# The last key search of a sparse attention cut into 18 pieces between its softmaxes, gate tiles moved into its rounds, scores issued in pairs

## What is computed

```python
h = rms_norm(x, g_mix[l]) * (1.0 + sc_m) + sh_m
qa, ka, va, qi, ki, wi, qb, kb, vb, ga, gb = split_cols(h @ w_in[l] + b_in[l])
# sparse attention: the 128 best keys of each query, by an index score, are kept
score = einsum('bqh,bqhs->bqs', wi, relu(qi . ki)) * INDEX_SCALE   # over 8 index heads
sel = top_k(where(admissible, score, -inf), 128)
y_a = softmax(qa . ka over sel) . va  @ w_oa[l]                    # 8 heads, one key/value head
# dense attention with a position bias, 8 heads of their own
y_b = softmax(qb . kb + bias) . vb  @ w_ob[l]
merged = sigmoid(ga) * y_a + sigmoid(gb) * y_b
x = x + gt_m * (merged @ w_out[l])
x = x + gt_f * ((silu(gate) * up) @ w_down[l])                     # gate, up = h2 @ w_gu[l]
```

## Time and profile before

| | us |
|---|---|
| median of 3 runs | 4437.27 (4436.09 to 4440.68) |
| the profiled execution, its own time | 4436.38 |
| its span, first to last instruction | 4434.6 |
| TensorE busy | 4012.5 (90%) |
| DVE / ACT / POOL busy | 1686.6 / 1419.9 / 1400.6 |
| first attention of the second block, layer 0 | 2718.4 to 2852.4 |
| second attention, layer 0 | 2852.4 to 2935.0 |
| first attention, layer 1 | 3667.4 to 3801.3 |

### The profile page before, as it was taken

One profiled execution on the slowest core, in us unless ns is written; L12 is line 12 of the kernel. 1 busy time (PEld: TensorE's weight loads), 2 busy tenths in 40 slices (PEclk: granted clock), 3 DMA queues, 4 the chain that ended last, 5 costly groups with the idle time before them and its releaser, 6 DMA issues.

```text
span 4434.6 us, 66065 instructions
## 1 busy us (share of the span) xinstructions
PE 4012.5 (90%) x28400; PEld 3192.3 (72%) x28400; DVE 1686.6 (38%) x2894; ACT 1419.9 (32%) x2412; POOL 1400.6 (32%) x583
## 2 busy tenths in 40 slices
PE   7798889989988987999899887999999887998999
PEld 5687568877866884678787675677787665787887
DVE  5443341466144444313562357223111475223112
ACT  3344152222223442433222233333222233433222
POOL 4000314344432002234344443023444432043443
PEclk9899899999988997999999997699999995899999
DMA  3001112256220001122363210112222220022222
GB/s 128 2 3 41 55 50 95 93 207 217 95 76 20 3 3 55 58 89 95 148 253 118 95 70 25 38 58 76 109 95 95 76 76 10 29 95 76 95 95 95
DMA packets 37147, 356.72 MB, mean 80 GB/s; under 512 B 4224, under 2 KB 4352, under 8 KB 17920
## 3 DMA queue, kind: packets, MB, share of 16 engines
q1 hardware_dynamic: 19584, 278.93, 16.9%
q10 hardware_dynamic: 17280, 73.60, 4.7%
HBM read 350.42 MB, written 2.10 MB: 79 GB/s over the span
## 4 chain that ended last, share of the span: by engine, by line
PE 80%; DVE 12%; ACT 3%; issue 2%; POOL 2%; DMA 1%; POOLq 0%; DVEq 0%; SPq 0%; PEldq 0%; ACTq 0%; PEld 0%
PE bank L658 20%; PE bank L659 20%; PE bank L660 20%; PE bank L987 11%; PE bank L1962 5%; PE bank L2049 1%; DVE arena L2400 1%; DVE arena L2399 1%; ACT arena L1317 1%; DMA ring<-stream 1%; DVE arena L1762 1%; DVE arena L1665 1%; ACT arena L2104 1%; POOL ring_r L746 1%; ACT hi_ring L737 1%
## 5 line engine op out<-in xcount | busy, mean ns | idle before, releaser
L746 POOL TENSOR_TENSOR ring_r<-ring,hi_ring 128x1024 fp32r<-128x1024 f32 (+1 forms) x522 | 1287.0, 2470 | 2579.5 <-ACT hi_ring L737 2579.4
L658 PE MATMUL bank<-xT_r,ring_r 128*128 128x512 f32 x2288 | 915.3, 400 | 22.9 <-DVE x_lo_r L2469 16.8
L659 PE MATMUL bank<-x_lo_r,hi_ring 128*128 128x512 f32 x2288 | 907.1, 396 | 0.0
L660 PE MATMUL bank<-xT_r,hi_ring 128*128 128x512 f32 x2288 | 903.6, 395 | 0.0
L737 ACT ACTIVATE hi_ring<-ring 128x1024 fp32r<-128x1024 f32 (+1 forms) x522 | 543.4, 1046 | 818.9 <-PE bank L660 392.5
L658 PEld LDWEIGHTS bank<-xT_r,ring_r 128*128 128x128 f32 x2288 | 436.7, 191 | 130.8 <-issue 30.6
L660 PEld LDWEIGHTS bank<-xT_r,hi_ring 128*128 128x128 f32 x2288 | 434.5, 190 | 101.8
L659 PEld LDWEIGHTS bank<-x_lo_r,hi_ring 128*128 128x128 f32 x2288 | 436.7, 191 | 96.6 <-issue 1.8
L987 PE MATMUL bank<-arena 64*64 64x64 f32 (+4 forms) x7456 | 394.6, 250 | 77.6 <-DVE arena L1665 29.6
L1317 ACT ACTIVATE arena<-bank 128x512 f32<-128x512 f32 (+1 forms) x422 | 230.4, 547 | 566.8 <-PE bank L660 359.8
L987 PEld LDWEIGHTS bank<-arena 64*64 64x64 f32 (+2 forms) x7456 | 306.0, 140 | 133.5 <-issue 90.7
(11 more groups left out here) (247 smaller groups left out, 5070.5 us busy)
## 6 DMA issues: line engine op xcount, KB each, us to landing
ring<-stream SPq DMA_DIRECT2D x132, 2048.0 KB, 7.8
arena<-ada ACTq DMA_DIRECT2D x96, 512.0 KB, 4.3
arena<-ln_rows ACTq DMA_DIRECT2D x5, 1024.0 KB, 7.6
arena<-edge ACTq DMA_DIRECT2D x4, 1024.0 KB, 5.0
arena<-edge ACTq DMA_DIRECT2D x2, 1792.0 KB, 7.4
arena<-pack ACTq DMA_DIRECT2D x2, 1548.0 KB, 6.5
arena<-pack ACTq DMA_DIRECT2D x2, 1200.5 KB, 12.7
x<-x_in SPq DMA_DIRECT2D x4, 512.0 KB, 7.3
```

The lines of the kernel that those rows point to most:

```text
L658: first = nc.tensor.matmul(out_, left[1], right[0], start=start, stop=False)
L659: low = nc.tensor.matmul(out_, left[0], right[1], start=False, stop=False)
L660: return first, low, nc.tensor.matmul(out_, left[0], right[0], start=False, stop=stop)
L746: nc.gpsimd.tensor_tensor(feed.raw(n, ring_r), feed.raw(n), feed.hi(n).bitcast(F32), ALU.subtract).then_inc(split_lo, 1)
```

## The change

- The search of the last query tile is cut into 18 pieces (`TOP_STEPS`: scaling, 16 pairs of MAX8 and replacement, mask). They are issued behind the softmaxes of turns 0 to 14 of the first attention, one or two to a turn. Tiles 1 and 2 are searched at one go as before, and the row steps behind them are 10 and 18 instead of 8 and 13, which leaves 8 instead of 15 behind the index scores of tile 3.
- A query tile's first softmax waits for the mask of its own tile instead of all four. ACT's squares of qb and kb wait for the last mask, since they overwrite the scores.
- The norm of qb moves to turns 17 and 18, that of kb to 25 and 27, the transposes of qb to 20, 21, 22 and 24, the load of the first half of the biases (`rel_half`) to turn 30.
- Six gate tiles are early: four in turns 2, 6, 10 and 14 of the first attention, two in turns 2 and 10 of the second. The `gt` steps go from the first attention behind gate tiles 4 to 7 of k = 1. The four `y2_split` steps go behind gate tiles 6 and 7 of k = 0, two each (they stood behind tiles 2 to 5, two of them thus ahead of tile 4).
- In both attentions score products come in pairs: rounds 0 and 1 at the start, then rounds n + 1 and n + 2 at the end of each odd turn n.
- Three regions of memory move with this, and the floor of the first gate piece's split is `idx(3, 0)` instead of `gt(0)`.

```diff
-EARLY_GATES = 4
+EARLY_GATES = 6
+TOP_STEPS = TOPK // 8 + 2
...
-        add("top", qt)
-        more((8, 13, len(rest))[qt - 1])
+        for i in range(TOP_STEPS if qt < TT - 1 else 0):
+            add("top", qt, i)
+        more((10, 18, len(rest))[qt - 1])
...
-        add("s_qk", a, 0, banks=(2,))
+        for n in range(2):
+            add("s_qk", a, n, banks=(2 + n,))
+        top = 0
         for n in range(TT * HQ + 3):
-            if n + 1 < TT * HQ:
-                add("s_qk", a, n + 1, banks=(2 + (n + 1) % 2,))
             if n < TT * HQ:
                 add("s_soft", a, n)
-            if a == 0 and n in (2, 12):
-                add("head_norm", ("qb", "kb")[n // 10], banks=("power",))
-            if a == 0 and n in (5, 15):
-                add("head_scale", ("qb", "kb")[n // 10])
+            while a == 0 and top < min(TOP_STEPS, TOP_STEPS * (n + 1) // (2 * HQ - 1)):
+                add("top", TT - 1, top)
+                top += 1
+            if a == 0 and n in (17, 25):
+                add("head_norm", ("qb", "kb")[n // 25], banks=("power",))
+            if a == 0 and n in (18, 27):
+                add("head_scale", ("qb", "kb")[n // 27])
...
-            if a == 1 and n in (1, 9, 17, 25):
-                add("gate", 0, n // 8, banks=(1,))
-            if a == 0 and n in (3, 5, 7, 14):
-                add("gt", (3, 5, 7, 14).index(n), banks=(1,))
-            if a == 0 and n in (8, 9, 10, 12):
-                add("rows_T", "qb", (8, 9, 10, 12).index(n), banks=(1,))
-            if a == 0 and n == 20:
+            if n in ((2, 6, 10, 14) if a == 0 else (2, 10)):
+                add("gate", 0, n // 4 + 4 * a - a * (n // 10), banks=(1,))
+            if a == 0 and n in (20, 21, 22, 24):
+                add("rows_T", "qb", (20, 21, 22, 24).index(n), banks=(1,))
+            if a == 0 and n == 30:
                 add("rel_half")
             if n >= 3:
                 add("s_pv", a, n - 3)
+            if n % 2 and n + 1 < TT * HQ:
+                for m in (n + 1, n + 2):
+                    add("s_qk", a, m, banks=(2 + m % 2,))
...
-            if n == 0 and dt in (2, 3, 4, 5):
-                add("y2_split", dt - 2)
+            if n == 0 and dt >= EARLY_GATES:
+                for c in range(2):
+                    add("y2_split", 2 * (dt - EARLY_GATES) + c)
+            if n == 1 and dt >= 4:
+                add("gt", dt - 4, banks=(1,))
...
-    return number(with_splits(out, second_pieces(), {24: ("gt", 0), GU_PIECE: ("turn2", 1, 2)}))
+    return number(with_splits(out, second_pieces(), {24: ("idx", 3, 0), GU_PIECE: ("turn2", 1, 2)}))
...
+                    act.wait_ge(mask_ready, TT)
...
-                    dve.wait_ge(mask_ready, TT)
                     drained(dve, uses, "rows_T", "misc", 1)
+                if h == 0 and a == 0:
+                    dve.wait_ge(mask_ready, qt + 1)
```

More of the change, by code:

```diff
@@ L1870, in build @@
     branch2_tmp = region(17200, 2)
-    gates2_early = [arena[:, a_:a_ + S] for a_ in (9232, 9744, W_HI + 4096, 12304)]
+    gates2_early = [arena[:, a_:a_ + S] for a_ in (3088, 3600, 4112, 4624, 12304, 9232)]
     def gate2_at(k, dt):
@@ L1888, in build @@
     mod_slot = [arena[:, 22888 + D * n:22888 + D * n + D] for n in range(MOD_SLOTS)]
-    gt_wide = arena[:, 12560:13072].rearrange("p (c q) -> p c q", c=4)
+    gt_wide = arena[:, 10256:10768].rearrange("p (c q) -> p c q", c=4)
     add_tmp = [arena[:, 5136:6160].rearrange("p (a c) -> p a c", a=2), xT[:, 0:D].rearrange("p (a c) -> p a c", a=2)]
@@ L2393, in step @@
             elif name == "top":
-                qt = args[0]
+                qt, i = args
                 w = (qt + 1) * P
-                link(V.tensor_scalar(score[:, 0:w], score[:, 0:w], INDEX_SCALE, None, ALU.mult))
-                link(V.memset(score[0:64, w - CH:w], NEG))
-                for _ in range(TOPK // 8):
+                if i == 0:
+                    link(V.tensor_scalar(score[:, 0:w], score[:, 0:w], INDEX_SCALE, None, ALU.mult))
+                    link(V.memset(score[0:64, w - CH:w], NEG))
+                elif i <= TOPK // 8:
                     link(V.max(out=top8, in_=score[:, 0:w]))
                     link(V.match_replace(out=score[:, 0:w], in_to_replace=top8, in_values=score[:, 0:w], imm_value=TAKEN))
-                link(V.tensor_scalar(score[:, 0:w], score[:, 0:w], TAKEN, -NEG, ALU.is_equal, ALU.mult))
-                V.tensor_scalar(mask[:, qt, 0:w], score[:, 0:w], NEG, None, ALU.add).then_inc(mask_ready, 1)
-                dve.wait_ge(mask_ready, qt + 1)
+                else:
+                    link(V.tensor_scalar(score[:, 0:w], score[:, 0:w], TAKEN, -NEG, ALU.is_equal, ALU.mult))
+                    V.tensor_scalar(mask[:, qt, 0:w], score[:, 0:w], NEG, None, ALU.add).then_inc(mask_ready, 1)
+                    dve.wait_ge(mask_ready, qt + 1)
             elif name == "s_soft":
```

## The result

| | before | after |
|---|---|---|
| median (lowest to highest) | 4438.98 (4436.09 to 4444.01), 4 runs | 4392.45 (4383.44 to 4399.9), 4 runs |
| ratio, 95% interval | | 0.9893 (0.9869 to 0.9917) |
| span of the profiled execution | 4434.6 | 4398.0 |
| forecast | | 4342, range 4298 to 4384 |

The kernel is 46.5 us faster, 23 a layer, where I had forecast 95, 47.6 a layer. The time lies outside the range. The profiled execution took 4399.9, 7.5 above the median.

What follows compares the result with a forecast made beforehand. Bound: TensorE's waits for DVE, then its low clock, around the first attention. Per layer 20.5 + 10 + 22 - 2.7 - 2.2 = 47.6, 95 for both layers; 4437.3 - 95.2 = 4342, range 4298 to 4384.

Steps and rivals of the forecast that it cites:

- The pairs of the second attention: Second attention: a score pair costs TensorE one single product; 16 pairs save 11.7 us, of which 10 taken, bounds 0 and 11.7.
- rival (c): Both attentions: pairs do not overlap, each waiting for its bank; 10 less and 9 less, 4380; chance with (b) 0.18.
- rival (d): Both attentions: sparse rounds fed by DVE never let the clock up, -24 us a layer, 4486, slower than before; chance 0.03.
- Ahead of the attention: Before the first attention: ten row steps fill 2.8 of a 3.9 us gap and avoid low clock; 7 us, bounds 3 and 9.
- Rounds 0 to 15: First attention up to softmax 16: 44.6 us plus 5 for clock falls between gate tiles; softmax 16 starts 22 us earlier.
- The rest of the first attention: From softmax 16 to the attention's end, at 1.2 GHz: 18.7 plus 52.2 us, thus 70.9 against 69.1 before.
- The time from softmax 16 to the end of the stall: First attention: qb's norm chain (squares, sum, POOL's power, scalings) gives TensorE its next work after 18.7 us, gap about 12.
- the stall of 2.7: Behind the second attention: y2_split 2 and 3 follow the last gate tile's tanh on ACT, branch(0, 0) waiting; costs 2.7 us.
- The pairs of the first attention: Behind the stall, at 1.2 GHz: each score pair costs one single product; without pairs, 9 us less gained.
- Rival (a): First attention behind the stall: the clock comes back, 50 us become 27, 18 a layer, 4306; halfway 4324; chance 0.27.
- kb's stall: First attention: kb's norm chain, about 15 us, hidden by slow rounds; if the clock returns it shows, some 5 us.
- the rule that I had set against the trace: Rest of the first attention: the skill says transposes do not engage full clock; by the trace they might lift it.

## Why the forecast was wrong

The experiments cut the miss of 24 a layer into three terms, by medians; they add up to 25, since each set of runs has its own median of the kernel before.

**The pairs of the second attention: forecast 10 gained, measured 4 lost.** This is the step that failed, 14 of the 24 (by the profiled executions, where the stage is 9.7 longer with pairs than without, nearly 20). I had taken the mean of 0.41 and 1.05 as saved per pair and multiplied by 16, and had looked for the limit in how long ACT and DVE need for a round. The limit is the order. Before, the bank of the next round was filled ahead of the softmax, so TensorE waited at most 0.8 us at a time, but for 1.3 at the very end; with pairs nine waits for ACT add up to 8.8, and at the lower clock the busy time that the pairs saved comes back. My rival (c), pairs that do not overlap, names the loss in the second attention for the wrong reason: they overlap, and they cost all the same. Four instructions of a pair take as long as two of a single one, in the kernel after:

```profile
2719.13 0.49 PE L1971 MATMUL bank<-arena 64*128 64x128 f32 x4
...
2720.11 0.48 PE L1971 MATMUL bank<-arena 64*128 64x128 f32 x2 [0.48 <-DVE small L2437]
```

"Sparse rounds fed by DVE never let the clock up" of rival (d) had the direction but was far too strong: in the changed kernel the clock came back within 17 us each time.

**Everything but the pairs: forecast 28.6, measured 17.2.** In the run without pairs, by stage and layer:
- Ahead of the attention I had 7 and it was 5.9 and 3.6 (85.5 and 85.6 to 79.6 and 82.0). In the changed kernel the first scores still left at 2719.1 and not at 2711.4, as the row steps ahead of this stage, which the change leaves alone, took 85.8 where they took 81.2 before.
- Rounds 0 to 15 take 55.1 and 54.9, where I had 44.6 + 5. The walk left out that POOL was still adding vb's bias: 4.2 of the 5.4 are the scaling beside it. In the changed kernel with pairs it is 59.2 and 57.4, as gate tiles started at 1.2 GHz in the gaps; I had allowed 5 for all four.
- The rest of the first attention, forecast 70.9 with pairs, thus 79.9 without, took 78.7 and 81.9. The time from softmax 16 to the end of the stall, forecast 18.7, was 18.4 in the changed kernel.
- The second attention without pairs took 71.2 and 71.1, forecast 82.6 - 11.0.
- Behind it, two gate tiles and the stall of 2.7 took 20.1, where 25.2 - 11.0 + 2.7 = 16.9 were due. The stall was there (2.67); the other 3.2 are the clock, 0.84 in the stretch of the changed kernel, which had fallen at the end of the attention. I had not priced a clock there.

**The pairs of the first attention: forecast 9, measured 9.3**, from 4402.7 to 4384.2, but the agreement is luck: it is the sum of errors. They cost 2.5 to 4.1 in rounds 0 to 15 and save 13 to 17 behind softmax 16 (78.7 and 81.9 to 65.2 and 64.6), which is 9.4 and 14.7 in the stage. I had counted 9 of array time there, at a clock held at 1.2 GHz by the trace of before; measured in layer 0, TensorE is busy for 44.2 us there where it was 67.0 without pairs, by the array time and the clock together, and idle for 9 more. Rival (a), that the pairs let the clock come back, had 0.27, and it happened in part: behind the stall the clock was 0.79 and 0.75, the stretch took 46.7 where I had 52.2 (and some 32 by the full rival), and kb's stall showed, as said there, by waits of 3.1 and 3.8. On the kernel before the same edit is worth 24 a layer. That was the largest single gain measured here, and I had it as 9.

One question was left from the prediction, the rule that I had set against the trace. The clock rose from 1.2 GHz in the old kernel at 2846 to 2848, 8.4 us behind the last score, which ended by 2838.6. In the kernel without pairs it rose 3.5 us behind the last single score (10.2 in layer 1), and in the one with the norms apart 6 us behind it, each time in a stretch of transposes and value products alone. The Trainium skill, page "TensorE: Matmul & The Clock Gate", section "Part 4: PE-mode transpose", has it that transposes do not bring full clock. These runs do not part transposes from the value products between them; together they ran up to each of these rises, though also for 10.2 us at 1.2 GHz ahead of one.

What stays open is why a stretch of single scores, busy without a break, keeps the low clock. That its products fill 64 of 128 rows, and pairs all of them, is a guess: no run had products of 128 rows in the order of single scores. Two traces speak against it as the whole cause. Paired rounds stayed at 1.2 GHz for 58 us in the run with no gate tile in the first attention, and in layer 1 of the old kernel with two gate tiles the clock rose as the last single score began and not behind it (that product, at 3787.05, took 1.12 us, as at 2.4 GHz); the first attention took 129.0 there and 133.9 in layer 0. Open too is what starts a fall in such a stretch: the same instructions with the same idle times kept the clock in one kernel and lost it in another.

The best version is the changed kernel with norm and scaling three and four turns apart, `y2_split` moved up, single scores in the second attention and gate tiles 2 and 4. It took 4358.5 and 4362.6 in two sets of runs, 81 and 77 below the kernel before, and in the first of them 35 below the changed kernel.

## What to carry to other kernels

A product that overlaps its neighbour can save nothing where it gives up the lead of one round: look at who issues ahead of whom before counting array time. Price a long stretch at its clock, not at its work: ask what in it went with a rise of a fallen clock before, and spread such blocks (here gate tiles) over it. And work moved into the gaps of another engine is free only if both run at once in the order as written; here DVE's search and the gate tiles took turns, and each gate tile kept most of its price.

## What was not expected of the hardware

- TensorE stayed at 1.2 GHz for 58 us with 58 us busy (x177), in rounds with one score product of 64 rows each, and went to 2.4 GHz 6 us behind the last of them. Another kernel, in rounds of pairs, stayed there for 58 us with 46.8 busy.
- A DVE scaling of 128x512 took 4.63 us instead of 0.43 beside a POOL addition of 4.50, and 3.85 when it started 1.03 us into it; a softmax of DVE beside the same addition (2718.42 in that kernel) kept its 0.28.
- One idle time of 0.36 us, the longest in 25 us, stood ahead of a fall of the clock in one kernel and ahead of none in another; the difference was 27 to 29 us in a stage of 70 to 72.
